# Hybrid trunk kernel on one core: delta decays from rows of running sums, the retention's normalised output ahead of the S5 rotations, the exponentials behind the second high part

## The reference, cut to what matters

```python
# gated DeltaNet, per head; g is the log decay of each position
gc = jnp.cumsum(g, axis=-1)
diff = gc[..., :, None] - gc[..., None, :]
decay = masked_exp(causal, diff)
a_mat = jnp.where(strict, einsum('bhnid,bhnjd->bhnij', kb, k) * decay, 0.0)
attn = einsum('bhnid,bhnjd->bhnij', q, k) * decay
...
# retention, per head
mu = jnp.mean(o, axis=-1, keepdims=True)
var = jnp.mean(jnp.square(o - mu), axis=-1, keepdims=True)
o = (o - mu) * lax.rsqrt(var + EPS)
```

## Time and profile before

| | |
|---|---|
| time, median of 3 runs | 2918.37 us (2918.34 to 2919.71) |
| time of the profiled execution | 2917.88 us |
| its span, first to last instruction | 2916.0 us |
| TensorE busy | 2869.0 us, 98% |
| VectorE busy | 1977.4 us, 68% |
| ScalarE busy | 1574.0 us, 54% |
| GpSimd busy | 422.3 us, 14% |
| DMA moved | 521.56 MB, mean 179 GB/s |

### The profile page before, as it was taken

One profiled execution on the slowest core, in us unless ns is written; L12 is line 12 of the kernel. 1 busy time (PEld: TensorE's weight loads), 2 busy tenths in 40 slices (PEclk: granted clock), 3 DMA queues, 4 the chain that ended last, 5 costly groups with the idle time before them and its releaser, 6 DMA issues.

```text
span 2916.0 us, 46745 instructions
## 1 busy us (share of the span) xinstructions
PE 2869.0 (98%) x17852; PEld 2562.9 (88%) x17852; DVE 1977.4 (68%) x3177; ACT 1574.0 (54%) x2401; POOL 422.3 (14%) x637
## 2 busy tenths in 40 slices
PE   7999999999999999999999999999999999999998
PEld 6899999999998888888889999999999888888887
DVE  6887788778875555555567877788778755555554
ACT  6556665666564444444556556655665644444443
POOL 3223132213200000000011332123211000000000
PEclk9999999999999999999999999999999999999999
DMA  6676677677766666666656766676667666666655
GB/s 163 163 172 166 175 181 174 164 177 179 175 175 195 194 194 195 193 192 185 192 129 165 178 171 174 172 179 171 171 171 181 181 195 195 192 192 195 194 180 166
DMA packets 636367, 521.56 MB, mean 179 GB/s; under 512 B 26480, under 2 KB 504496, under 8 KB 635760
## 3 DMA queue, kind: packets, MB, share of 16 engines
q1 hardware_dynamic: 612944, 483.46, 59.1%
q0 software_dynamic: 22816, 34.00, 6.8%
q10 hardware_dynamic: 384, 1.11, 0.1%
HBM read 487.02 MB, written 2.10 MB: 168 GB/s over the span
## 4 chain that ended last, share of the span: by engine, by line
PE 65%; issue 26%; DVE 4%; ACT 2%; DVEq 1%; POOL 1%; DMA 1%; ACTq 0%; POOLq 0%
PE PJ L1794 42%; PE S L1794 16%; PE RA L1794 3%; PE GB L1794 2%; DVE mix L1367 1%; DVE w_lo L1223 1%; POOL gnorm L585 0%; POOL w_lo L500 0%; DVE region L1402 0%; ACT w_lo L649 0%; DVE region L1404 0%; DVE region L1405 0%; DVEq L1406 0%; DVE region L1412 0%; DVEq L1413 0%
## 5 line engine op out<-in xcount | busy, mean ns | idle before, releaser
L1223 DVE TENSOR_TENSOR w_lo<-raw_w,w_hi 128x1024 fp32r<-128x1024 f32 (+1 forms) x912 | 1055.3, 1160 | 757.3 <-ACT w_hi L651 729.9
L651 ACT ACTIVATE w_hi<-raw_w 128x1024 fp32r<-128x1024 f32 x912 | 962.5, 1058 | 791.4 <-PE PJ L1794 342.5
L1794 PE MATMUL PJ<-h_hi,w_hi 128*128 128x256 f32 x2560 | 744.7, 291 | 1.6 <-DMA w_lo<-raw_w 1.6
L1794 PE MATMUL PJ<-h_hi,w_lo 128*128 128x256 f32 x2560 | 724.5, 283 | 0.0
L1794 PE MATMUL PJ<-h_lo,w_hi 128*128 128x256 f32 x2560 | 724.3, 283 | 0.0
L1794 PEld LDWEIGHTS PJ<-h_hi,w_hi 128*128 128x128 f32 x2560 | 490.4, 192 | 9.7 <-issue 6.8
L1794 PEld LDWEIGHTS PJ<-h_lo,w_hi 128*128 128x128 f32 x2560 | 490.6, 192 | 0.0
L1794 PEld LDWEIGHTS PJ<-h_hi,w_lo 128*128 128x128 f32 x2560 | 489.9, 191 | 0.0
L1794 PE MATMUL PJ<-w_hi,h_hi 128*128 128x512 f32 x1152 | 461.5, 401 | 1.9 <-DVE h_lo L1698 1.9
L1794 PE MATMUL PJ<-w_hi,h_lo 128*128 128x512 f32 x1152 | 450.4, 391 | 0.0
L1794 PE MATMUL PJ<-w_lo,h_hi 128*128 128x512 f32 x1152 | 449.9, 391 | 0.0
(11 more groups left out here) (386 smaller groups left out, 3988.6 us busy)
## 6 DMA issues: line engine op xcount, KB each, us to landing
raw_w<-w_in SPq DMA_DIRECT2D x576, 512.0 KB, 3.9
raw_w<-w_in SPq DMA_DIRECT2D x512, 128.0 KB, 2.7
raw_w<-w_branch SPq DMA_DIRECT2D x128, 512.0 KB, 4.2
raw_w<-w_out SPq DMA_DIRECT2D x64, 512.0 KB, 4.1
w_lo<-raw_w POOLq DMA_DIRECT2D x112, 256.0 KB, 4.3
raw_w<-s_glu_w SPq DMA_DIRECT2D x16, 512.0 KB, 4.5
ret_decay<-c_ret POOLq DMA_DIRECT2D x16, 128.0 KB, 3.8
out<-x_tok SPq DMA_DIRECT2D x4, 512.0 KB, 4.0
```

Of the source, the lines that this page charges most:

```text
L651: A_(w_hi[i % RING][:, :, :], raw_w[i % RING][:, :, :], ACT.Copy).then_inc(hi_ready, 1)
L1223: TT(w_lo[i % RING][:, 0:ks, :], raw_w[i % RING][:, 0:ks, :], w_hi[i % RING][:, 0:ks, :].bitcast(f32), ALU.subtract).then_inc(raw_used[i % ...
L1794: return nc.tensor.matmul(o, w, m, start=start, stop=stop)
```

## The change

- TensorE: g_decay_t and g_decay_s (five products) are replaced by g_rows (two products). The running sums gc of each block come as rows, the same in each of the 128 partitions: a tile with g in every column, times `upto`. g_rows stands ahead of project(1), at u = 0 behind project(5).
- ScalarE: spread_gates writes two tiles of ones times g instead of three tiles.
- VectorE: a new step decay_logs makes the five 128x128 logs from the two rows and the column of running sums, with a subtraction or an addition and a minimum or maximum with 0, and stores them in dec_t and dec_s. It stands behind ret_variance, at u = 0 behind s5_add(1).
- ScalarE: one step decays takes the exponentials of dec_t (384 columns) and dec_s (256 columns, with scale -1) in place. It stands behind ahead(2), at u = 0 behind ahead(5).
- VectorE: ret_normalize moves from behind s5_turn(0) to behind decay_logs, ahead of s5_turn(0).
- GpSimd's list is as it was. GB is written three times a unit instead of four.

```diff
-GA_N, GB_N, HA_N, RA_N, SA_N = 20, 4, 11, 3, 4
+GA_N, GB_N, HA_N, RA_N, SA_N = 20, 3, 11, 3, 4
...
                 def spread_gates(v):
 
                     for a in range(2):
-                        A_(g_later[:, a, :], after, ACT.Copy, scale=gate_g[:, a, ds(v, 1)])
-                    A_(g_bc, ones[:, :], ACT.Copy, scale=gate_g[:, 1, ds(v, 1)])
+                        A_(g_wide[:, a, :], ones[:, :], ACT.Copy, scale=gate_g[:, a, ds(v, 1)])
                     act.drain().then_inc(spread_ready, 1)
...
-                    def decays_t():
-                        act.wait_ge(gb_w, gb0 + 1)
-                        A_(dec_t[:, 0:3:2, :], GB[:, 0:2 * P].rearrange("p (a n) -> p a n", a=2), ACT.Exp).then_inc(dec_raised, 1)
-                        A_(dec_t[:, 1, :], GB[:, 2 * P:3 * P], ACT.Exp, bias=unit_cols[:, u, C_SUF0:C_SUF0 + 1]).then_inc(gb_r, 1)
-
-                    def decays_s():
-                        act.wait_ge(gb_w, gb0 + 2)
-                        A_(dec_s[:, :, :], GB[:, 0:2 * P].rearrange("p (a n) -> p a n", a=2), ACT.Exp).then_inc(gb_r, 1)
+                    def decays():
+
+                        act.wait_ge(dec_logs, n1)
+                        A_(dec_t[:, :, :], dec_t[:, :, :], ACT.Exp).then_inc(dec_raised, 1)
+                        A_(dec_s[:, :, :], dec_s[:, :, :], ACT.Exp, scale=-1.0).then_inc(dec_s_ready, 1)
...
                         ahead(5)
-                        act.wait_ge(gdn_qkv_used, n1)
-                        decays_t()
+                        decays()
                         if n == 0:
                             stage_bc()
                         ahead(6)
-                        decays_s()
                         silu_conv(1, gq2)
...
                         stage_u()
                         ahead(1)
-                        act.wait_ge(gdn_qkv_used, n1)
-                        decays_t()
                         ahead(2)
-                        decays_s()
+                        decays()
                         stage_conv(B_GK, 0)
...
+                    def decay_logs():
+
+                        dve.wait_ge(gb_w, gb0 + 1)
+                        for a in range(2):
+                            row, at = GB[:, a * P:(a + 1) * P], unit_cols[:, u, C_GC0 + a:C_GC0 + a + 1]
+                            TS(dec_t[:, 2 * a, :], row, at, 0.0, ALU.subtract, ALU.min)
+                            TS(dec_s[:, a, :], row, at, 0.0, ALU.subtract, ALU.max)
+                        TS(dec_t[:, 1, :], GB[:, P:2 * P], unit_cols[:, u, C_SUF0:C_SUF0 + 1], None, ALU.add).then_inc(
+                            gb_r, 1)
+                        dve.drain().then_inc(dec_logs, 1)
+
...
                         if n:
                             s5_add(1)
+                        decay_logs()
                         bounds()
...
                         ret_variance(u - 1)
+                        decay_logs()
+                        ret_normalize(u - 1)
                         dve.wait_ge(sincos_ready, n1)
                         s5_turn(0)
-                        ret_normalize(u - 1)
                         ahead(2)
...
-                    dve.wait_ge(gb_r, gb0 + 3)
+                    dve.wait_ge(dec_s_ready, n1)
...
-                    def g_decay_t():
-
-                        pe.wait_ge(cols_ready, l1)
+                    def g_rows():
+
                         pe.wait_ge(spread_ready, n1)
                         pe.wait_ge(gb_r, gb0 + 1)
                         for a in range(2):
-                            MM(GB[:, a * P:(a + 1) * P], g_later[:, a, :], upto)
-                        MM(GB[:, 2 * P:3 * P], g_bc, upto).then_inc(gb_w, 1)
-
-                    def g_decay_s():
-                        pe.wait_ge(gb_r, gb0 + 2)
-                        for a in range(2):
-                            last = MM(GB[:, a * P:(a + 1) * P], upto, g_later[:, a, :])
+                            last = MM(GB[:, a * P:(a + 1) * P], g_wide[:, a, :], upto)
                         last.then_inc(gb_w, 1)
...
                         project(5)
-                        g_decay_t()
+                        g_rows()
                         if l == 0:
                             s_turn()
                         project(6)
-                        g_decay_s()
                         if l == 0:
                             s_bu(0)
...
                         g_turn(u - 1)
+                        g_rows()
                         project(1)
-                        g_decay_t()
                         r_out(u - 1)
                         project(2)
                         s_bu_all()
-                        g_decay_s()
                         project(3)
```

More of the change, by code:

```diff
@@ L255, in trunk_kernel @@
         gate_s = mix[:, :, :].rearrange("p (a b) n -> p a (b n)", a=2)
-        g_later = in_work(2, P)
-        g_bc = sq[:, 2, :]
+        g_wide = in_work(2, P)
         dec_t = in_work(3, P)
@@ L381, in trunk_kernel @@
         spread_ready, dec_raised, dec_masked = sem("spread_ready"), sem("dec_raised"), sem("dec_masked")
+        dec_logs, dec_s_ready = sem("dec_logs"), sem("dec_s_ready")
         conv_staged, conv_summed, conv_done = sem("conv_staged"), sem("conv_summed"), sem("conv_done")
@@ L925, in _ @@
                     act.drain().then_inc(ha_r, 1)
-                    act.wait_ge(gb_w, gb0 + 4)
+                    act.wait_ge(gb_w, gb0 + 3)
                     for a in range(2):
@@ L1515, in _ @@
                         s5_add(1)
-                    dve.wait_ge(gb_w, gb0 + 3)
+                    dve.wait_ge(gb_w, gb0 + 2)
                     TS(gnorm[:, :], GB[:, 0:4], EPS, None, ALU.add).then_inc(gb_r, 1)
@@ L1935, in g_norms @@
                         pe.wait_ge(conv_done, cv0 + 2)
-                        pe.wait_ge(gb_r, gb0 + 3)
+                        pe.wait_ge(gb_r, gb0 + 2)
                         for m, t in enumerate((gk2, gq2)):
@@ L1944, in g_gram_k @@
                         if n:
-                            pe.wait_ge(sa_r, sa0 + 3)
+                            pe.wait_ge(sa_r, sa0 + 4)
                         for a in range(2):
@@ L1951, in g_values @@
                         pe.wait_ge(conv_done, cv0 + 3)
-                        pe.wait_ge(gb_r, gb0 + 4)
+                        pe.wait_ge(gb_r, gb0 + 3)
                         for a in range(2):
```

## The result

The changed kernel took **2994.57 us** (median of four runs, 2991.39 to 2996.55) against 2918.73 us (2918.34 to 2919.71) for the kernel before in the same session: a ratio of 1.026, 95% interval 1.0246 to 1.0274. That is slower, 76 us of it, inside the range given and 12.6 us above the forecast of 2982.0 us.

A forecast was written before the change was run, and what follows sets the result against it. TensorE, 98% busy, was taken as bound together with a VectorE and ScalarE chain. Chain 52.6, first units 3 and clock 8 gave 63.6 us on 2917.88; with 0.5 for the median, 2982.0 us, own range 2968 to 2997, wider range 2948 to 2998.

The forecast's parts named there:

- TensorE's own pace and VectorE's chain end together, so the chain is paid in full: Units with u > 0: a later VectorE chain delays everything, 3.76 us a unit, 52.6 us over 14 units.
- The root hangs on the mask, the mask on the exponential behind the second high part: GpSimd's unchanged order: the root ends at 159.32 us, so the normalisation, wanted at 156.6, starts at 159.37.
- The logs are covered: VectorE's five logs, 1.6 us, fit while it waits for the root; uncovered, rotations would start about 1 us later.
- faster, the other side: Rival: root ready by 156.6 us, rotations keep their start, TensorE's saving counts, 2907 us; chance 0.05.
- TensorE's shorter queue: Ten TensorE records a unit become four: at most 0.66 us a unit, 9.2 us over 14 units.
- Waits of 1.8 us at the transpose and 2.6 us at the sums of squares: New TensorE idle times in each of 14 units, before the retention's transpose and before the gram sums of squares.
- No drain behind the table load: ScalarE: exponential starts 1.30 us behind the 1.28 us load's start; a 1.38 us drain would have added 19 us.
- The first units cost 3 us: Units with u = 0: logs behind the S5 sums cost layer 1 2.9 us, layer 0 nothing; bounds -1 and +4.
- The clock falls at one wait in three, 8 us: TensorE's granted clock drops behind 5 of 14 waits, 1.5 us each: +8 us, bounds 0 and 21.
- upper bound of 21: Top of the clock term: TensorE's clock falls in all 14 units, 1.5 us each.
- more: Rival: clock falls behind each long wait and some short ones, or the load drains: 2998 to 3015 us; chance 0.06.
- caught up in part: Rival: VectorE's idle time before the second low part absorbs some delay: 2955 us, or 2935 us; chance 0.11.

The follow-up runs named there:

- e1: Changed kernel with GpSimd's retention root put ahead of the mask of dec_t: 2954.23 us.
- e2: Changed kernel with ret_normalize put back behind the rotations, s5_turn(0), on VectorE: 2939.02 us.
- e6: Changed kernel with logs in VectorE's earlier idle time, exponentials early, root before mask, normalisation behind ahead(3), transpose behind project(5): 2909.57 us.
- e7: Kernel before, own five products kept, with only the normalisation moved behind ahead(3) and the retention's transpose behind project(5): 2914.94 us.
- e4: Changed kernel with unread products of constant tiles filling TensorE's wait ahead of the sums of squares: 2974.48 us.
- e8: Changed kernel with the root ahead of the mask, as in e1, and the normalisation back behind s5_turn(0): 2936.78 us.
- e10: Changed kernel, in units with u = 0 only: logs behind conv_taps(1), silu_conv(1) ahead of the exponentials: 2989.71 us.
- e3: Changed kernel with the exponentials put back ahead of the second high part, ahead(2), on ScalarE: 2981.97 us.
- e9: e6 with silu_conv(1) ahead of the exponentials and the high part in units with u = 0: 2907.26 us.

## Why the prediction was right, point by point

- **TensorE's own pace and VectorE's chain end together, so the chain is paid in full.** Right. The low part is 3.63 us late (3.76 forecast), the idle time before the second low part absorbed nothing, and e1 and e2, which move one link each, bring the delay down to 0.73 and 0.98 us a unit. Term: 50.8 us where 52.6 stood.
- **The root hangs on the mask, the mask on the exponential behind the second high part.** Right in each link. With the 1.06 us taken off, the exponential starts at 157.13 us (157.14 forecast) and takes 0.53 us (0.52), the root starts 0.69 us behind the mask (0.88), the normalisation starts at 159.16 us (159.37). The 0.88 us between mask and root before was no cost of the pair: the root waited there for the variance, which ended at 154.47 us. With the variance long done the two follow each other without a gap. That misreading of the earlier trace rows is worth 0.2 us; with 0.08 us more between the normalisation and the low part, the chain came out 0.13 us shorter than forecast.
- **The logs are covered.** Right where they were priced: five in 1.40 us with starts 0.26 us apart (0.33 forecast), done by 157.2 us, 3.0 us ahead of the root. But the forecast's price of 1 us with the cover gone is what e1 shows: once the root is early, the logs and the normalisation make VectorE 0.73 us late, and "faster, the other side" does not come by mending GpSimd alone. Its figure of 2907 us rested on an early root being enough; e1 has it early and is at 2954. The 9.2 us at which TensorE's shorter queue was priced are borne out only in e6 against e7, with VectorE's order changed as well.
- **Waits of 1.8 us at the transpose and 2.6 us at the sums of squares.** Right: 1.63 and 2.54 us.
- **No drain behind the table load.** Right: the exponential starts 1.30 us behind the start of the load of 1.28 us (156.89 to 158.19). The Trainium skill, "ScalarE: Activation LUTs", section "What ACT_TABLE_LOAD costs", puts a drain of 1.38 us behind the load; by this row there is none.
- **The first units cost 3 us.** The step was mis-sized: 7.6 us. The mechanism of layer 1, the logs behind the S5 sums, is there with its forecast 2.9 us (from TensorE's gate sums to its sums of squares 16.91 us instead of 14.00). But TensorE stands for 6.21 us at one place, and from 1550.7 to 1561.0 us, the last 2.3 us of this wait and 7.9 us behind it, the clock is at 0.50, which no term had. The other 3.6 of the 6.5 us of layer 1 fall behind the sums of squares, and are put down to this low clock. Layer 0, taken as nothing, is 1.1 us.
- **The clock falls at one wait in three, 8 us.** This is the term that was wrong. It was sized on one unit of one stretch: three idle times, one of them with a low clock behind the earlier trace rows. The place of the wait was not asked. The clock fell at 14 of 14 waits before the one-column products and at none before the transpose; it cost 1.3 us a unit, a little under the 1.5 us that the earlier trace rows gave, so 18.4 us where 8 stood, near the upper bound of 21. Of the miss of 13 us, 10 are here, 5 in the first units, and -2 in the chain. The share of one in three had nothing to stand on but those three idle times.

The rival "more" had its condition fulfilled in the main: the clock fell at each of the 14 longer waits, before the sums of squares, though at none of the shorter ones before the transpose. With the upper bound of 21 us for these falls in place of the 8, the forecast's own sum is 2995.0 us, and 2994.57 were measured, nearer than the forecast. That closeness is luck, since the first units cost 4.6 us more than in that sum and clock and chain 4.4 us less. The rival "caught up in part" is out, by the 1.31 us that stayed.

What stays open is what decides whether the clock falls at a wait. In the units with u > 0 the traces have 70 waits of 1.38 to 1.75 us before the transpose (the changed kernel, e2, e4, e8, e10), and it fell at none; of 56 waits of 1.48 to 2.90 us before the sums of squares (the changed kernel, e1, e3, e10) it fell at 52. Length alone does not part them. The one-column products behind the wait are not the whole reason either: in the second unit of the changed kernel the clock was down before the first of them started. In the first unit of layer 1 of e9 it fell at a wait of 3.10 us ahead of 256-column products (0.55 behind it), while in e10 it stayed up behind a wait of the same length at the same place. What TensorE did ahead of the wait was not varied by any experiment.

## What to carry to other kernels

An engine that is 98% busy may still be paced by another chain that ends at the same moment; look for the local chain of waits in one period before counting on instructions taken away, and look on every engine's queue at what stands ahead of the small instruction that the moved one needs. Here an unchanged pair of lines on GpSimd, mask before root, turned the move of one exponential into 3.6 us a unit. Price an expected wait of TensorE twice, once as time and once as the granted clock at it, and count how many times per run it comes. Where it can't be taken away, try another place for it (e8) or products to fill it (e4): here both kept the clock up, though no run shows what makes one place better than another.

## What the hardware showed that was not expected

- The granted clock fell to 0.5 at 52 of 56 waits of 1.48 to 2.90 us before eight one-column products, and at none of 70 waits of 1.38 to 1.75 us before a transpose with projections behind it; the difference between two kernels with the same delay of the chain (e1 and e8) was 17.5 us.
- Ten products that nobody reads (20 records, 2.40 us of TensorE in each unit with u > 0, and 24 products in the first unit of layer 1) made a kernel 20 us faster.
- A VectorE instruction that reads 128x128 from a bank with a column scalar takes 0.34 us, and in the run of five logs the next starts 0.26 us behind it.
- ScalarE's table load did not wait for what its activation waited for. In the first unit of layer 1 of the changed kernel the load starts right behind ScalarE's last instruction, and the exponential starts 4.57 us after the load did:

```profile
1543.93 1.28 ACT L756 ACT_TABLE_LOAD   x1
1548.50 0.52 ACT L756 ACTIVATE work<-work 128x384 f32<-128x384 f32 x1 [3.28 <-DVEq L1469]
```
